# The modulation's matrix-vector product: TensorE in the sparse attention, or scaled adds on VectorE in the first feed-forward

## What is computed

```python
def second_block(x, c, w_ada, b_ada, ...):
    c_act = jax.nn.silu(c)
    mod = c_act @ w_ada[l] + b_ada[l]          # 1024 times 1024x6144
    sh1, sc1, gt1, sh2, sc2, gt2 = jnp.split(mod, 6, axis=-1)
    h = _modulate(_rmsnorm(x, g_mix[l]), sh1, sc1)
    x = x + gt1[:, None, :] * _mixer(h, ...)
    h = _modulate(_rmsnorm(x, g_ffn[l]), sh2, sc2)
    a = jnp.square(jax.nn.relu(jnp.einsum('bsd,df->bsf', h, w_ff1[l])))
    x = x + gt2[:, None, :] * jnp.einsum('bsf,fd->bsd', a, w_ff2[l])
```

## Time and profile before

| | |
|---|---|
| median of 3 runs | 3115.86 us (3112.82 to 3118.89) |
| span of the profiled execution | 3116.1 us |
| TensorE busy | 2836.1 us, 91% |
| VectorE busy | 1455.1 us, 47% |
| ScalarE busy | 932.0 us, 30% |
| POOL busy | 263.3 us, 8% |

### The profile page before, as it was taken

How to read it: one execution, slowest core, us unless ns; L and a number is a source line. 1 busy time by engine, 2 the same in 40 slices (tenths; PEclk the granted TensorE clock), 3 DMA queues, 4 the chain that set the end, 5 groups by cost and what they waited for, 6 DMA issues and landing times.

```text
span 3116.1 us, 36793 instructions
## 1 busy us (share of the span) xinstructions
PE 2836.1 (91%) x13150; PEld 2272.7 (73%) x13150; DVE 1455.1 (47%) x2871; ACT 932.0 (30%) x1906; POOL 263.3 (8%) x430
## 2 busy tenths in 40 slices
PE   4976879996999799999999989998898999999997
PEld 4745758883567678888888867777776888888886
DVE  5274569996433333233322353333843444433445
ACT  5154342222220132222222244223414222222222
POOL 0221411221004100000000000002200000000000
PEclk9988969997999899999999989999888999999999
DMA  4011022333634302011111112221040201110111
GB/s 156 19 31 50 28 62 76 103 101 113 221 116 154 124 20 81 28 54 54 54 37 43 54 44 89 69 74 49 15 169 11 77 28 54 54 54 27 54 40 61
DMA packets 119645, 213.99 MB, mean 69 GB/s; under 512 B 10852, under 2 KB 39100, under 8 KB 119284
## 3 DMA queue, kind: packets, MB, share of 16 engines
q1 hardware_dynamic: 107188, 185.30, 18.2%
q10 hardware_dynamic: 8064, 14.68, 1.3%
q0 software_dynamic: 4288, 12.64, 1.2%
HBM read 178.94 MB, written 33.64 MB: 68 GB/s over the span
## 4 chain that ended last, share of the span: by engine, by line
PE 70%; DVE 13%; issue 7%; ACT 5%; DMA 3%; POOL 2%; SPq 0%; DVEq 0%; ACTq 0%
PE bank L1594 20%; PE bank L1595 19%; PE bank L1596 19%; PE bank L1820 3%; DVE w_lo L980 1%; ACT w_hi L600 1%; PE bank L1807 1%; PE bank L1785 1%; DVE cmpj L1184 1%; DVE stage L1272 1%; DVE probs L1085 1%; DMA w_raw<-in_w_ff 1%; PE bank L1795 1%; DMA w_raw<-in_w_in 1%; DVE mx L1071 1%
## 5 line engine op out<-in xcount | busy, mean ns | idle before, releaser
L1594 PE MATMUL bank<-h_hi,w_hi 128*128 128x512 f32 (+1 forms) x1312 | 513.1, 391 | 18.5 <-DVE h_lo L1386 7.9
L1595 PE MATMUL bank<-h_lo,w_hi 128*128 128x512 f32 (+1 forms) x1312 | 510.6, 389 | 0.0
L1596 PE MATMUL bank<-h_hi,w_lo 128*128 128x512 f32 (+1 forms) x1312 | 510.3, 389 | 0.0
L600 ACT ACTIVATE w_hi<-w_raw 128x512 fp32r<-128x512 f32 (+3 forms) x440 | 255.0, 616 | 762.4 <-PE bank L1596 550.3
L1594 PE MATMUL bank<-w_hi,hid_hi 128*128 128x512 f32 x1024 | 400.2, 391 | 8.2 <-DVEq L1345 8.0
L1595 PE MATMUL bank<-w_lo,hid_hi 128*128 128x512 f32 x1024 | 398.5, 389 | 0.0
L1596 PE MATMUL bank<-w_hi,hid_lo 128*128 128x512 f32 x1024 | 398.4, 389 | 0.0
L980 DVE TENSOR_TENSOR w_lo<-w_raw,w_hi 128x512 fp32r<-128x512 f32 (+3 forms) x384 | 246.6, 679 | 205.8 <-ACT w_hi L600 199.1
L1318 DVE TENSOR_TENSOR hid_lo<-bank,hid_hi 128x512 fp32r<-128x512 f32 x128 | 88.5, 692 | 510.4 <-ACT hid_hi L805 510.4
L1594 PEld LDWEIGHTS bank<-h_hi,w_hi 128*128 128x128 f32 x1312 | 248.7, 190 | 73.7 <-DVE h_lo L1386 8.7
L1595 PEld LDWEIGHTS bank<-h_lo,w_hi 128*128 128x128 f32 x1312 | 248.7, 190 | 51.0 <-issue 0.7
(11 more groups left out here) (374 smaller groups left out, 4004.0 us busy)
## 6 DMA issues: line engine op xcount, KB each, us to landing
w_raw<-in_w_ff SPq DMA_DIRECT2D x128, 256.0 KB, 3.0
w_raw<-in_w_in SPq DMA_DIRECT2D x104, 256.0 KB, 3.0
ada<-in_w_ada SPq DMA_DIRECT2D x24, 1024.0 KB, 5.3
w_raw<-in_w_mlp_in SPq DMA_DIRECT2D x64, 256.0 KB, 3.0
w_raw<-in_w_mlp_out SPq DMA_DIRECT2D x64, 256.0 KB, 3.0
gates_scratch<-gstage ACTq DMA_DIRECT2D x48, 256.0 KB, 2.0
stage<-gates_scratch SPq DMA_DIRECT2D x16, 768.0 KB, 5.1
w_raw<-in_w_out SPq DMA_DIRECT2D x32, 256.0 KB, 3.6
```

What stands on the lines that cost most here:

```text
L600: A_(W[par][0][:, p, 0:n], raw[:, p % NRAW, 0:n], ACT.Copy).then_inc(w_hi, 1)
L1594: mm(out, lh, rh, start=(i == 0), stop=False)
L1595: mm(out, lh, rl, start=False, stop=False)
L1596: last = mm(out, ll, rh, start=False, stop=(i == n - 1))
```

## The change

The 24 products leave TensorE's loop of the sparse attention, and with them the 24 loads on SP, the wide copy of `silu(c)`, the addition of the bias rows and the transposes. Instead the matrix-vector product is made in the first feed-forward, in the second halves of chunks 1 to 6, four blocks of 256 columns in each chunk:

- POOL issues 96 loads of 256 KB (two slices of 128 rows by 256 columns), into two buffers; a load waits until the two steps that read the buffer before are done.
- VectorE does 32 steps per chunk, behind its adds: three each behind u = 0 and 1, two behind u = 2 to 14. A step is `ada_sum = w * silu(c)[k] + ada_sum` on 128 x 256 (the first of a block a multiplication). There is one `ada_sum`; the first step of a block waits until TensorE has read it.
- TensorE, behind its groups u = 3, 7, 11 and 15, waits for the 8 steps of the block and sums `ada_sum` over the 128 partitions, with two matmuls of one column against a vector of ones, into bank 4.
- At the end VectorE adds the bias, which comes with the other small vectors, and writes `modc`. POOL stores the two gate rows from it.

The `oT` loads are issued at once by SP. TensorE's last chunk is written out, since it has no modulation.

```diff
--- before.py
+++ after.py
@@ SBUF tensors @@
-        adab = [at("ada0", [P, 8, 256], f32, s3 + 10240), at("ada1", [P, 8, 256], f32, t3 + 6144)]
-        NPC = 24
-        cwide = at("silu_c_wide", [P, 8, 2 * NPC - 1], f32, s2 + 23040)
...
+        ROW0 = mcur[0] - 4096
+        adab = [at(f"ada{i}", [P, 2, 256], f32, ROW0 + 2048 * i) for i in range(2)]
+        adac = at("ada_sum", [P, 256], f32, ROW0 - 1024)
@@ block.sync @@
-                                     ("g_head_2", c_ghead, 4), ("pool_scale_2", c_pool, 4), ("c_2", c_c, 8)):
+                                     ("g_head_2", c_ghead, 4), ("pool_scale_2", c_pool, 4), ("c_2", c_c, 8),
+                                     ("b_ada_2", c_ada, 48)):
...
-            for n in range(24):
-                if n >= 2:
-                    sp.wait_ge(ada_mm, n - 1)
-                elif n == 1:
-                    sp.wait_ge(sel_done, 6)
-                sp.dma_start(adab[n % 2][:, :, :], ada[:, :, n * 256:(n + 1) * 256]).then_inc(ada_in[n % 2], 16)
-                if n >= 3 and attended:
-                    h, o, d, k0, k1 = attended.pop(0)
-                    sp.dma_start(o[:, k0:k1, :].bitcast(f32), d[k0 * P:k1 * P, h * HALF:(h + 1) * HALF]
-                                 .rearrange("(k p) q -> p k q", p=P)).then_inc(o_in, 16)
+            for h, o, d, k0, k1 in attended:
+                sp.dma_start(o[:, k0:k1, :].bitcast(f32), d[k0 * P:k1 * P, h * HALF:(h + 1) * HALF]
+                             .rearrange("(k p) q -> p k q", p=P)).then_inc(o_in, 16)
...
-                    sp.wait_ge(ada_mm, 24)
+                    sp.wait_ge(sel_done, 6)
@@ block.gpsimd @@
-            pool.wait_ge(d_s, 24)
-            pool.dma_start(brows[:, :], a["b_ada_2"][0].rearrange("(n c) -> n c", c=256)).then_inc(b_in, 16)
-            pool.wait_ge(ada_r, 1)
-            pool.dma_start(mod_d, mrows[:, :]).then_inc(mod_out, 16)
...
             pool.wait_ge(d_pv, 32)
+            ada = a["w_ada_2"][0].rearrange("(k p) n -> p k n", p=P)
+            for q in range(96):
+                n, k = q // 4, 2 * (q % 4)
+                if q >= 2:
+                    pool.wait_ge(ada_s, 2 * q - 2)
+                pool.dma_start(adab[q % 2][:, :, :], ada[:, k:k + 2, n * 256:(n + 1) * 256]).then_inc(ada_in[q % 2], 16)
+            pool.wait_ge(ada_s, 192)
             row(rowv, a["g_final"].rearrange("(o n) -> o n", o=1))
+            pool.wait_ge(ada_ok, 1)
+            with nc.allow_non_contiguous_dma(reason="two rows of the modulation, from columns"):
+                for k in (16, 40):
+                    pool.dma_start(mod_d[k:k + 8, :].rearrange("k p -> p k"), modc[:, k:k + 8]).then_inc(mod_out, 16)
...
-            pool.wait_ge(mod_out, 16)
+            pool.wait_ge(mod_out, 32)
             row(rowv, mod_row(2))
@@ block.vector @@
-            link(nc.vector.memset(cwide[:, :, :], 0.0))
-            tt(cwide[:, :, NPC - 1], cact[:, :], cols[:, c_c:c_c + 8], ALU.mult).then_inc(ada_c, 1)
+            link(tt(cact[:, :], cact[:, :], cols[:, c_c:c_c + 8], ALU.mult))
+            link(nc.vector.memset(one[:, :], 1.0))
...
-            dve.wait_ge(ada_mm, NPC)
-            dve.wait_ge(b_in, 16)
-            tt(mrows[:, :], bank[3][0:NPC, 0:256], brows[:, :], ALU.add).then_inc(ada_r, 1)
-            dve.wait_ge(ada_t, 1)
-            nc.vector.tensor_copy(modc[:, :].rearrange("p (n j) -> p j n", j=2),
-                                  bank[3][:, 0:48].rearrange("p (j n) -> p j n", j=2)).then_inc(ada_ok, 1)
...
-                if n == 1:
-                    dve.wait_ge(mod_out, 16)
...
+                def modulation(i, r):
+
+                    n, k = r // 8, r % 8
+                    q = r // 2
+                    x = adab[q % 2][:, k % 2, :]
+                    if k % 2 == 0:
+                        dve.wait_ge(ada_in[q % 2], i * 128 + (16 * (q // 2 + 1) - 128))
+                    if k == 0:
+                        dve.wait_ge(ada_mm, i * 4 + (n - 3))
+                        l = tsc(adac[:, :], x, cact[:, 0:1], None, ALU.mult)
+                    else:
+                        l = stt(adac[:, :], x, cact[:, k:k + 1], adac[:, :], ALU.mult, ALU.add)
+                    l.then_inc(ada_s, 1)
+                    dve.wait_ge(ada_s, i * 32 + (r + 1 - 32))
...
                             dve.sem_inc(group_free, 1)
+                            if not k and not first and not last:
+                                u = 2 * t + m
+                                for r in range(2 * u + min(u, 2), min(32, 2 * u + 2 + min(u + 1, 2))):
+                                    modulation(i, r)
...
+            dve.wait_ge(ada_mm, 25)
+            tt(modc[:, :], bank[4][:, 0:48], cols[:, c_ada:c_ada + 48], ALU.add).then_inc(ada_ok, 1)
+            dve.wait_ge(ada_ok, 1)
@@ block.tensor @@
-            pe.wait_ge(ada_c, 1)
+            pe.wait_ge(is_s, len(ISC))
...
-                if 8 <= u < 32:
-                    n = u - 8
-                    pe.wait_ge(ada_in[n % 2], 16 * (n // 2 + 1))
-                    for k in range(8):
-                        l = mm(bank[3][0:NPC, 0:256], cwide[:, k, NPC - 1 - n:2 * NPC - 1 - n], adab[n % 2][:, k, :],
-                               start=(n == 0 and k == 0), stop=(n == NPC - 1 and k == 7))
-                    l.then_inc(ada_mm, 1)
...
-            pe.wait_ge(ada_r, 1)
-            for j in range(2):
-                l = nc.tensor.transpose(bank[3][:, j * NPC:(j + 1) * NPC], mrows[:, j * P:(j + 1) * P], ident[0:NPC, 0:NPC])
-            l.then_inc(ada_t, 1)
...
-            pe.wait_ge(ada_ok, 1)
...
+                def modulation(i, n):
+
+                    pe.wait_ge(ada_s, i * 32 + (8 * n + 8 - 32))
+                    for e in range(2):
+                        l = mm(bank[4][:, ds(i * 8 + (2 * n + e - 8), 1)], adac[:, e * P:(e + 1) * P], one[:, :],
+                               start=True, stop=True)
+                    l.then_inc(ada_mm, 1)
...
+                            if not k and not first and not last and (2 * t + m) % 4 == 3:
+                                modulation(i, t // 2)
...
-                with pe.Fori(1, FC) as i:
-                    chunk(i, False)
+                with pe.Fori(1, FC - 1) as i:
+                    chunk(i, False, False)
+                chunk(FC - 1, False, True)
...
-            norm_transposes
+            pe.wait_ge(ada_ok, 1)
             norm_transposes(40, 18, 0)
```

More of the change, by code:

```diff
@@ L37, in build @@
     x1_d = nc.dram_tensor("x1_scratch", (P, NT, D), f32).ap()
-    mod_d = nc.dram_tensor("mod_scratch", (24, 256), f32).ap()
+    mod_d = nc.dram_tensor("mod_scratch", (48, P), f32).ap()
     rows_d = nc.dram_tensor("rows_scratch", (2, 8, S), f32).ap()
@@ L98, in build @@
         zero = misc("zero", [P, 1])
+        one = misc("one", [P, 1])
         bg_now = misc("bg_now", [P, 8])
@@ L108, in build @@
             0, 8, 16, 40, 48, 56, 64, 68, 72
-        NV = 80
+        c_ada = 80
+        NV = 128
         hT = [act_pair("hT0", s0), act_pair("hT1", s1)]
@@ L156, in build @@
         oT = [act_pair("oT0", s0), act_pair("oT1", s1)]
-        adab = [at("ada0", [P, 8, 256], f32, s3 + 10240), at("ada1", [P, 8, 256], f32, t3 + 6144)]
-        NPC = 24
-        cwide = at("silu_c_wide", [P, 8, 2 * NPC - 1], f32, s2 + 23040)
-        mrows = at("mod_rows", [NPC, 256], f32, s2 + 19968)
-        brows = at("mod_bias_rows", [NPC, 256], f32, s2 + 20992)
+        ROW0 = mcur[0] - 4096
+        adab = [at(f"ada{i}", [P, 2, 256], f32, ROW0 + 2048 * i) for i in range(2)]
+        adac = at("ada_sum", [P, 256], f32, ROW0 - 1024)
         mT = [act_pair("mT0", s2), act_pair("mT1", s3)]
@@ L236, in build @@
         bg_ok = sem("bg_ok")
-        ada_r, ada_t = sem("ada_rows"), sem("ada_tr")
         chain = sem("chain")
@@ L244, in build @@
         sel_done = sem("sel_done")
-        ada_in, ada_mm, ada_e, ada_c, ada_ok = [sem("ada_in0"), sem("ada_in1")], sem("ada_mm"), sem("ada_e"), sem("ada_c"), sem("ada_ok")
+        ada_in, ada_s, ada_mm, ada_e, ada_ok = [sem("ada_in0"), sem("ada_in1")], sem("ada_sum"), sem("ada_mm"), sem("ada_e"), sem("ada_ok")
         o_in = sem("o_in")
@@ L263, in build @@
         y_sg = [sem("y_sg0"), sem("y_sg1")]
-        gt_x, b_in, mod_out = sem("gt_x"), sem("mod_bias_in"), sem("mod_out")
+        gt_x, mod_out = sem("gt_x"), sem("mod_out")
         out_done = sem("out_done")
@@ L333, in _ @@
             load_chunk(C_PD, wide(a["w_proj_dsa"][0], 0, 2) + wide(a["w_proj_mem"][0], 0, 2))
-            ada = a["w_ada_2"][0].rearrange("(k p) n -> p k n", p=P)
             for b in range(2):
@@ L522, in mod_row @@
             def mod_row(k):
-                return mod_d.rearrange("(s r) c -> s (r c)", r=4)[k:k + 1, :]
+                return mod_d.rearrange("(s r) c -> s (r c)", r=8)[k:k + 1, :]
             pool.wait_ge(d_pv, 32)
+            ada = a["w_ada_2"][0].rearrange("(k p) n -> p k n", p=P)
[5 more added lines that the diff above has]
+            pool.wait_ge(ada_s, 192)
```

(23 more changed lines are left out.)

## The result

The changed kernel took 3121.12 us (median of 20 runs, 3118.78 to 3126.67), the kernel before 3116.98 in 20 runs beside it. The ratio is 1.0015, with a 95% interval of 1.0009 to 1.0022: 4 to 5 us slower, within the 0.2% that the prediction calls no change, where it had forecast 7 us less. The span of the profiled execution is 3120.1 us, 4.0 more than before.

The account below looks back on a forecast made before the run. TensorE was taken as the bound, busy 91% of the 3116.1 us span. The sum was 3116.1 − 80.7 gained + 72.8 added + 0.55 for small additions = 3108.8 us, range 3093 to 3135.

Parts of the forecast that it names:

- the clock's give-back in the sparse attention: Sparse attention: without the first product, small matmuls of a unit and a half more run at half clock, 2.9 us lost.
- The second rival: Sparse attention: the clock does not rise, the remaining 83 us take twice as long, 3185 us in all; chance 0.04.
- The other give-backs: Sparse attention: 3.3 us for waits on the splitting of outputs and 1.2 us for jitter between TensorE and VectorE.
- outputs' hand-over: Sparse attention: the next block's `dsa_out` waits until ScalarE and VectorE split the outputs, 0.55 us six times, 3.3 us.
- jitter: Sparse attention, blocks 2 to 4: TensorE and VectorE take nearly equal time per unit, so 1.2 us is allowed.
- the 1.1 us at the merge: End of the sparse attention: the merge need not wait for the rows and their transposes, 1.1 us gained.
- the memset: Ahead of the search: the memset of the wide copy goes from VectorE, 0.3 us gained.
- The steady part: Feed-forward second halves: VectorE needs 2.02 us per group, TensorE 2.72, so waits at a chunk's later three blocks cost nothing.
- The first block: Feed-forward, first block of each of six chunks: TensorE waits 8.0 us for VectorE's adds and steps and the loads.
- The half pace behind the wait: Feed-forward, behind the first block's wait: matmuls run 4.4 us at half pace, 2.2 us lost per chunk.
- the two sums: Feed-forward: TensorE's two products with one column, summing `ada_sum`, cost 0.48 us per block.
- The first rival: Feed-forward: the round trip of loads through POOL is longer than 3.6 us, each further microsecond costing 6 us; chance 0.12.

Follow-up runs that it names:

- the first and the last row of the table: Changed kernel with later sums and eight useless matmuls at u = 8, 3065.75 us; with later sums, even steps and four at u = 6, 3054.46 us.

## Why the prediction was wrong

It forecast a gain of 80.7 us and a cost of 73.3, net 7 us less. The time lies inside its range of 3093 to 3135, but on the other side of no change. (Its sums start from a span, which in the executions on record is 1.8 to 2.3 us below the time; the differences are not touched by that.) The profile has 74.3 gained (up to the first transposes of the feed-forward, 1129.10 against 1054.79) and 77.3 lost in the feed-forward, and 1 us in all that follows.

- **The step that failed is the clock's give-back in the sparse attention**, put at 2.9 us, "a unit and a half". It was some 7 units long, up to 785 us. From the distances above: 100.3 us in the changed kernel, 86.7 with the clock up, so 13.7 us. That is 10.8 too little in the sum. The second rival named this mechanism, with its all-or-nothing price of 83 us and a chance of 0.04; it came in part, since the clock rose by itself at 785 us. In all six traces without a burst that held, it rose within the first two units of block 4, whose scores need a second matmul; that the longer units raise it is an inference. The argument against the rival, that TensorE would be busy without a gap, did not hold: it was busy 15.00 of 15.00 us twice, at 0.50. The row that should have weighed more is the 0.50 at 60% busy: the window at 205 us showed only that a clock that is up can stay up.
- **The other give-backs** (outputs' hand-over 3.3, jitter 1.2) were 3.0 together, if the 1.1 us at the merge are taken as forecast: from 755.58 to 927.04 before is 171.5 us, less 86.7 for the products 84.8, less 1.1 for the merge 83.7; with the clock up 86.7 remained. 1.5 us better than predicted.
- **Ahead of that point** the changed kernel is 2.9 us earlier (752.65 against 755.51, the start of the first product), where 0.3 had been forecast for the memset. The same point lies between 750.2 and 755.7 us in the 13 traces, so this part lies within the spread of the traces, and no run shows an effect behind it.
- **The steady part** was right: steps of 0.49 and 0.35 us, 2.04 us per group in the trace without the loads (adds at 1220.43 and 1222.47), no wait at the second, third and fourth blocks.
- **The first block** was right in mechanism and size: 8.2 us of idle time, 7.9 less today's stall, against 8.0. The round trip was 3.4 us (freed at 1219.33, issued at 1219.62, used at 1222.76), against 3.6. The half pace behind the wait cost 1.4 to 2.4 us (7 to 12 matmuls at 0.20 us more), against 2.2; the two sums at half clock cost 1.2 instead of 0.5, the others 0.45 each against 0.48. Per chunk 12.25 us, against 10.7 + 1.4 = 12.1; in the run without the product 72.3 us in all, against 72.8.
- **The first rival** did not come: the loads landed 3.1 us after their issue, though POOL needed 0.72 us for one instead of 0.56. What the Trainium skill says in "SBUF — State Buffer", section "Who interferes with whom", of POOL's descriptors beside a `tensor_scalar` was not tested: none of the 96 issues in the trace overlapped one of these steps.
- **A part that had no term**: chunk 0. Its first halves took 23.50 and 23.37 us instead of 21.90 each, 3.1 us lost at half pace, with similar idle times ahead of them (2.25 and 1.56 us, before 1.57 and 1.98). Nine of the eleven experiments' traces have this too. The two with the first halves at 21.9 (the first and the last row of the table) run the same instructions there as the nine, with idle times of 1.81 and 1.98 us. That it is chance at which moment the idle times fall is an inference; no run moved the moment alone.

Together: 10.8 for the clock, less 1.5 for the other give-backs, less 2.6 for the earlier start, less 0.3 between merge and feed-forward; then 3.1 for chunk 0, 1.5 for the rest of the feed-forward (0.7 in the second halves, 0.8 in first halves of 43.65 instead of 43.52 us), and 0.4 behind it, where 1.0 stands against 0.55. That is 11.4 us, the distance between −7.4 and +4.0. With the clock's term right, the forecast would have been about 3120.

## What to carry to other kernels

Where an engine's work is moved under another's, ask at which point the receiving engine is late in its own loop: here VectorE had 171.5 us of room in the feed-forward, and a result wanted behind the fourth group cost 8 us per chunk, behind the seventh almost nothing. Work that is taken off TensorE can take the full clock with it: here what was left kept TensorE busy and still did not bring the clock up for 30 us, and 3.0 us of useless work at the right place, with no long idle time behind it, gave back 13.7.

## What the runs showed of the hardware

TensorE was busy without a gap from 755 to 785 us at half clock and did not get the full one. With a burst of 3.0 us (four fp32 matmuls of 256 columns, or 16 transposes of 128) the granted clock rose and stayed; with 1.05 us (one trace) it did not. Behind the burst an idle time of 0.62 us (ahead of 762.53 with the burst at u = 8) left it up, one of 4.42 us (burst at u = 1) brought it down, as did 8 us in every chunk. Reads of 256 KB in rows of 1 KB by POOL landed in 3.1 us beside a busy VectorE, nearly as fast as SP's of 2 KB rows (3.0).
